# The last two output chunks of a hybrid attention layer as a pair in seven block products

## What is computed

```python
def hybrid_layer(x, cos, sin, w_in, ...):
    h = rmsnorm(x, g_norm)
    proj = jnp.einsum('bsd,de->bse', h, w_in)
    ...
    y_moba = rmsnorm(o_moba * jax.nn.silu(m_z), g_out_moba)
    ...
    y_nsa = rmsnorm(o_nsa * jax.nn.silu(n_z), g_out_nsa)
    y = jnp.concatenate([y_moba, y_nsa], axis=-1)
    return x + jnp.einsum('bse,ed->bsd', y, w_out)

def reference(x, ...):
    x = hybrid_layer(...)
    return rmsnorm(x, g_final)
```

## Time and profile before

| | before |
|---|---|
| median of 3 runs | 498.31 us |
| lowest, highest | 498.20, 498.56 us |
| the profiled execution | 498.54 us |
| its span | 496.7 us |
| matmuls and transposes in the program of TensorE | 1947 rows of its order |
| TensorE busy | 487.2 us (98%) |
| VectorE busy | 335.6 us (68%) |
| ScalarE busy | 250.5 us (50%) |
| GpSimd busy | 60.9 us (12%) |
| read from HBM | 93.93 MB |

### The profile page before, as it was taken

One profiled execution on the slowest core, in us unless ns is written; L12 is line 12 of the kernel. 1 busy time (PEld: TensorE's weight loads), 2 busy tenths in 40 slices (PEclk: granted clock), 3 DMA queues, 4 the chain that ended last, 5 costly groups with the idle time before them and its releaser, 6 DMA issues.

```text
span 496.7 us, 6459 instructions
## 1 busy us (share of the span) xinstructions
PE 487.2 (98%) x2512; PEld 405.4 (82%) x2512; DVE 335.6 (68%) x535; ACT 250.5 (50%) x358; POOL 60.9 (12%) x66
## 2 busy tenths in 40 slices
PE   8999999999999999999999999999999999999993
PEld 7888788787788888888888888888888888888882
DVE  5887544345879948766587878666888766765442
ACT  5884335353556535544544464665664544545421
POOL 2340101000102202000020200000323131022020
PEclk9999999999999999999999999999999999999998
DMA  8989788585353452443443734346257577367222
...
DMA packets 54543, 96.45 MB, mean 194 GB/s; under 512 B 4368, under 2 KB 13168, under 8 KB 54128
## 3 DMA queue, kind: packets, MB, share of 16 engines
...
HBM read 93.93 MB, written 2.10 MB: 193 GB/s over the span
## 4 chain that ended last, share of the span: by engine, by line
PE 95%; issue 2%; DMA 1%; DVE 0%; ACT 0%; ACTq 0%; POOLq 0%; POOL 0%; DVEq 0%
PE proj L647 26%; PE proj L649 25%; PE proj L648 25%; PE b_o L941 4%; PE b_t L628 2%; PE b_p L910 2%; PE b_s L810 2%; PE proj L680 2%; PE proj L686 1%; PE proj L691 1%; DMA xo<-in_x_dram 1%; PE b_s L649 1%; PE b_s L647 1%; PE b_s L648 1%; PE b_p L628 0%
## 5 line engine op out<-in xcount | busy, mean ns | idle before, releaser
L1341 DVE TENSOR_TENSOR w_lo<-w_raw,w_hi 128x2048 fp32r<-128x2048 f32 x68 | 157.5, 2319 | 87.6 <-ACT w_hi L1018 87.4
L647 PE MATMUL proj<-w_hi,xT_hi 128*128 128x512 f32 x484 | 191.0, 395 | 0.0
L649 PE MATMUL proj<-w_hi,xT_lo 128*128 128x512 f32 x484 | 188.8, 390 | 0.0
L648 PE MATMUL proj<-w_lo,xT_hi 128*128 128x512 f32 x484 | 188.6, 390 | 0.0
L1018 ACT ACTIVATE w_hi<-w_raw 128x2048 fp32r<-128x2048 f32 x68 | 129.7, 1911 | 34.9 <-PE proj L649 24.5
L647 PEld LDWEIGHTS proj<-w_hi,xT_hi 128*128 128x128 f32 x484 | 90.9, 188 | 20.1 <-issue 1.6
L649 PEld LDWEIGHTS proj<-w_hi,xT_lo 128*128 128x128 f32 x484 | 90.9, 188 | 19.4
L648 PEld LDWEIGHTS proj<-w_lo,xT_hi 128*128 128x128 f32 x484 | 91.0, 188 | 17.8
L1155 ACT ACTIVATE pT<-b_p 128x512 f32<-128x512 f32 (+2 forms) x24 | 11.7, 489 | 53.9 <-PE b_p L910 53.9
L595 POOL TENSOR_TENSOR rope_a<-rope_a,rope_b 128x512 f32<-128x512 f32 (+1 forms) x12 | 13.1, 1109 | 160.8 <-DVE rope_b L1428 160.8
L647 PE MATMUL proj<-w_hi,ymT_hi 128*128 128x512 f32 x80 | 31.2, 390 | 0.0
...
## 6 DMA issues: line engine op xcount, KB each, us to landing
...
```

Source lines behind the costliest of these rows:

```text
L647: nc.tensor.matmul(dst, a_hi, b_hi, start=first, stop=False, skip_group_check=goes_on)
L648: nc.tensor.matmul(dst, a_hi, b_lo, start=False, stop=False, skip_group_check=goes_on)
L649: return nc.tensor.matmul(dst, a_lo, b_hi, start=False, stop=last, skip_group_check=goes_on)
L1341: nc.vector.tensor_tensor(wl, w_raw[:, u % RAW], wh.bitcast(F32), ALU.subtract).then_inc(lo_ready, 1)
```

## The change

Output chunks 2 and 3 become the third pair. Their first units (2, 0) and (3, 0), 48 matmuls, are replaced by seven block products of 6 matmuls, with sums of y's blocks in the place of x's. For that, chunk 0's last unit moves ahead of both of chunk 1's; the blocks of the weights are loaded by SyncE, rounded by ScalarE and VectorE; y's sums are formed by VectorE in slot 60 (`y_sums`), rounded by ScalarE in slot 62 (`ys_round`) and their lo made by VectorE in slot 64 (`ys_residual`). The four copies of banks go to `rope_b` and `prob`, and VectorE adds them to the sum in memory (`mid_add`). `last_chunk` keeps the two units (3, 2) and (3, 3). Cut to its core:

```diff
-OUT_UNITS = [(0, 0), (0, 1), (1, 0), (1, 1), (0, 2), (1, 2), (0, 3), (1, 3)] + [(c, g) for c in (2, 3) for g in range(4)]
+OUT_UNITS = [(0, 0), (0, 1), (1, 0), (1, 1), (0, 2), (0, 3), (1, 2), (1, 3)]
+NSLOT = NPROJ + 16
+OUT_DONE = [65, 67, 71]
+PAIRS = [(11, 12), (13, 14), (NC + 2, NC + 3)]
+Z_PAIRS = 2
+FIRST_BLOCKS, T2_SLOT, EARLY, MIDDLE_BLOCKS, LATE_BLOCKS = [40, 48, 65], [41, 49, 66], [42, 50, 66], [42, 50, 67], [43, 51, 68]
+MIDDLE, LATE = [44, 52, 68], [45, 53, 69]
...
-    for c, g in OUT_UNITS:
+    for c, g in OUT_UNITS[:-1]:
         plain(NC + c, g)
+    a, b = PAIRS[2]
+    ring.append(("early", 2))
+    plain(NC + OUT_UNITS[-1][0], OUT_UNITS[-1][1])
+    ring.append(("middle", 2))
+    plain(a, 1)
+    ring.append(("late", 2))
+    for c, g in ((a, 2), (a, 3), (b, 1), (b, 2), (b, 3)):
+        plain(c, g)
...
+              66: 63, 67: 64, 68: 65, 69: 66, 70: 67, 71: 68, 72: 69}
...
+        ys = raw_e[:, :, :].rearrange("p m c -> p (m c)").rearrange("p (k t) -> p k t", k=UK)
+        ys_hi, ys_lo = xT_hi[:, NH:NH + UK, :], xT_lo[:, NH:NH + UK, :]
...
+                if u == 61:
+                    sp.wait_ge(blk_lo, 14)
+                    block(2, 0)
+                    block(2, 1)
+                if u == 63:
+                    block(2, 3)
+                if u == 65:
+                    sp.wait_ge(xs_lo_ok, 2)
+                    block(2, 2)
...
-                pe.wait_ge(xs_lo_ok, 1)
+                pe.wait_ge(xs_lo_ok, 1 if p < Z_PAIRS else 2)
...
-                bank_free(NC + 3)
                 for m in range(MT):
-                    for g in range(UPC):
+                    for u in (NU - 2, NU - 1):
...
+            def ys_round():
+                act.wait_ge(xs_ok, 2)
+                act.wait_ge(unit_used, used(UNIT_NO[NC - 1, 2]))
+                nc.scalar.activation(ys_hi, ys, ACT.Copy).then_inc(xs_hi_ok, 1)
...
+                if p == 2:
+                    act.wait_ge(y_done, 8)
+                    nc.scalar.activation(mid_copy(p, i), mid_bank(p, i)[:, :], ACT.Copy).then_inc(mid_out, 1)
+                    return
...
+                    if slot == MIDDLE[p]:
+                        if p == 2:
+                            block_hi(p, 4)
+                            block_hi(p, 5)
                         mid_out_(p, 2)
...
+            def mid_add(i):
+                m, c = ((0, 3), (1, 2), (0, 2), (1, 3))[i]
+                dve.wait_ge(mid_out, 4 * 2 + i + 1)
+                a = acc[:, m, c * CW:(c + 1) * CW]
+                nc.vector.tensor_tensor(a, mid_copy(2, i), a, ALU.add).then_inc(mid_added, 1)
+            def y_sums():
+                dve.wait_ge(ylo_done, 2)
...
+                step(nc.vector.tensor_tensor(ys, ymT_hi[:, 0:UK, :].bitcast(F32), ymT_lo[:, 0:UK, :].bitcast(F32), ALU.add), 5)
+                step(nc.vector.tensor_tensor(d, c, d, ALU.add), 6)
+                step(nc.vector.tensor_tensor(c, a, c, ALU.subtract), 7)
+                step(nc.vector.tensor_tensor(a, d, a, ALU.subtract), 8)
+                nc.vector.tensor_tensor(b, b, a, ALU.subtract).then_inc(xs_ok, 1)
...
+                if slot == LATE_BLOCKS[2]:
+                    block_lo(2, 4)
+                    block_lo(2, 5)
...
+                if slot == 60:
+                    y_sums()
+                if slot == MIDDLE_BLOCKS[2]:
+                    t4(2)
+                for i, at in enumerate((68, 68, 69, 70)):
+                    if slot == at:
+                        mid_add(i)
```

More of the change, by code:

```diff
@@ L78, in stream @@
     plain(first - 1, 3)
-    for p, (a, b, _) in enumerate(PAIRS):
+    for p, (a, b) in enumerate(PAIRS[:Z_PAIRS]):
         ring.append(("middle", p))
@@ L124, in rounded_at @@
         return slot + 2
-    return ROUNDED_AT.get(slot) if slot < 60 else slot - 2
-OUT_SLOT = OUT_DONE[:2] + [OUT_DONE[2] + 2]
+    return slot - 2 if 60 <= slot < 65 else ROUNDED_AT.get(slot)
+OUT_SLOT = OUT_DONE
 RAW, SPL = 3, 3
@@ L727, in seven @@
                 pe.wait_ge(blk_lo, 7 * p + n + 1)
-                xh, xl = [t[:, k0:k0 + 2, m * P:(m + 1) * P] for t in (xT_hi, xT_lo)] if of == "x" else                          [t[:, m, k0:k0 + 2, :] for t in (xs_hi, xs_lo)]
+                if of == "s" and p < Z_PAIRS:
+                    xh, xl = [t[:, m, k0:k0 + 2, :] for t in (xs_hi, xs_lo)]
+                else:
+                    pair = (ys_hi, ys_lo) if of == "s" else (xT_hi, xT_lo) if p < Z_PAIRS else (ymT_hi, ymT_lo)
+                    xh, xl = [t[:, k0:k0 + 2, m * P:(m + 1) * P] for t in pair]
                 wh, wl = block_split(p, n)
@@ L757, in last_chunk @@
             def last_chunk():
[L759 removed]
                 for m in range(MT):
[L761 removed]
+                    for u in (NU - 2, NU - 1):
                         if m == 0:
[L763 removed]
+                            pe.wait_ge(lo_ready, u - FIRST + 1)
                         for k in range(UK):
[L765 removed]
+                            last = three_products(*operands(u, m, k), False, u == NU - 1 and k == UK - 1, True)
                     last.then_inc(last_done, 1)
@@ L970, in _ @@
                 for p in range(len(PAIRS)):
-                    if slot == PAIRS[p][2] - 2:
+                    if slot == EARLY[p] and p < Z_PAIRS:
                         pair_early(p)
-                    if slot == PAIRS[p][2]:
+                    if slot == MIDDLE[p]:
                         pair_middle(p)
-                    if slot == PAIRS[p][2] + 1:
+                    if slot == LATE[p]:
                         pair_late(p)
@@ L978, in _ @@
                     unit(unit_at(slot))
+                if slot == EARLY[2]:
+                    pair_early(2)
                 if slot == 2:
@@ L1239, in _ @@
                     xs_round()
+                if slot == 62:
+                    ys_round()
                 for p in range(len(PAIRS)):
-                    s0 = PAIRS[p][2]
-                    if slot == s0 - 4:
+                    if slot == FIRST_BLOCKS[p]:
                         block_hi(p, 0)
                         block_hi(p, 1)
-                    if slot == s0 - 2 and p:
+                    if slot == MIDDLE_BLOCKS[p] and p:
                         block_hi(p, 2)
@@ L1290, in _ @@
                     prob_out(JOB_AT[slot - 2])
-                for p in range(len(PAIRS)):
-                    if slot == PAIRS[p][2] - 1:
-                        block_hi(p, 4)
-                        block_hi(p, 5)
+                if slot in LATE_BLOCKS[:Z_PAIRS]:
+                    for n in (4, 5):
+                        block_hi(LATE_BLOCKS.index(slot), n)
                 if slot % UPC == UPC - 1 and slot < NPROJ and ACT_READS[KINDS[slot // UPC]]:
@@ L1689, in _ @@
                     xs_residual()
+                if slot == 64:
+                    ys_residual()
                 for p in range(len(PAIRS)):
-                    s0 = PAIRS[p][2]
-                    if slot == s0 - 4:
+                    if slot == FIRST_BLOCKS[p]:
                         block_lo(p, 0)
@@ L1743, in _ @@
                     row_max(JOB_AT[slot])
-                for p in range(len(PAIRS)):
-                    if slot == PAIRS[p][2] - 1:
-                        block_lo(p, 4)
-                        block_lo(p, 5)
+                if slot in LATE_BLOCKS[:Z_PAIRS]:
+                    for n in (4, 5):
+                        block_lo(LATE_BLOCKS.index(slot), n)
                 if slot % UPC == UPC - 1 and slot < NPROJ and KINDS[slot // UPC] == "z":
```

71 lines of the change are left out of this document (39 added, 32 removed).

## The result

| | before | with the change |
|---|---|---|
| median | 498.33 us (4 executions) | 503.86 us (4 executions) |
| lowest, highest | 498.20, 498.56 us | 503.71, 503.88 us (the other three) |
| TensorE busy | 487.2 us | 487.8 us |
| VectorE busy | 335.6 us | 351.7 us |
| ScalarE busy | 250.5 us | 256.5 us |

The ratio is 1.0109, with a 95% interval of 1.0090 to 1.0129: 5.5 us slower, where 6.7 had been forecast (505.0, range 500 to 508).

The account below looks back on a forecast made before the run. TensorE, busy 98% of the span, was taken to bound the kernel; -1.36 us for six matmuls, five waits, restarts, 0.58 for GpSimd and 0.8 for y's sums made +6.7 us: 498.31 to 505.0 us, range 500 to 508.

Parts of the forecast that it names:

- first wait: Ahead of unit (0, 3), now a slot earlier: TensorE waits 1.13 us for the last part of y.
- y's sums: VectorE's slot 60: five sums, held up by GpSimd, make the last part of y 0.8 us late (0 to 1.35).
- second wait: Ahead of unit (1, 3): its hi stands behind ScalarE's squares of chunk 0, so TensorE waits 0.81 us.
- third wait: Ahead of unit (2, 1): its lo comes after TensorE wants it, a wait of 0.17 us.
- fourth wait: Ahead of P7: fifth block's lo and P6's copy come late, the largest wait, 3.15 us.
- fifth wait: Ahead of P4: the seventh block's lo ends after TensorE wants it, a wait of 0.91 us.
- restarts: TensorE after each of five waits: the second matmul starts later than usual, costing 0.11 us each.
- rival 3: TensorE's clock falls in the wait ahead of P7; slow matmuls cost 1.5 to 3 us more, 507.3; chance 0.13.
- the tail after the last matmul is the same work as before: After TensorE's last matmul: the remaining work is unchanged, so no time is added or taken away.
- the squares stand in front of the fifth block: ScalarE's program order: squares of chunk 1 run 454.53 to 456.08, ahead of the fifth block's rounding, ending 457.22.
- GpSimd's 0.58: Fifth block's lo on VectorE: GpSimd's second multiplication for chunk 1 keeps it waiting 0.58 us (0 to 0.58).
- What would show it: Signs in the trace: TensorE's busy time falls, five gaps appear, the first of y's sums takes 2.3 us.

Follow-up runs that it names:

- e9_as_is_again: The change unaltered, timed in more rounds beside the kernel with 16 added matmuls; 503.75 us, its profiled execution 503.89 us.
- e8_all: The change with y's second-half factor on ScalarE, both chunks' squares later, VectorE's block lo's and chunk 1's sums earlier; 496.60 us, 0.9966 of before.
- e6: On top of e2, the norm's factor on y's second half moved from VectorE's slot 61 to ScalarE's slot 62; 500.80 us.
- e2: The change with ScalarE's squares of chunk 1 moved behind the fifth and sixth block's roundings and P6's copy; 502.12 us.
- e7: On top of e2, ScalarE's squares of chunk 0 moved behind the hi of unit (1, 3); 500.16 us.
- e10_fill_again: The change with 16 matmuls that nobody reads in TensorE's wait ahead of P7, second timing; 502.81 us.
- e1_as_is: The change unaltered, for a second look at its trace; 504.55 us, its profiled execution 505.20 us.

## Why the prediction was right, and where it was not

The forecast of 505.0 against 503.86 comes from the right mechanism, but a part of the agreement is luck: terms that were too large stand against a fall of the clock that the sum did not have. Step by step, from the distances of starts in e9_as_is_again:

| term | forecast | measured |
|---|---|---|
| six matmuls less | -1.36 | -1.36 (e8_all: -1.5 of busy time) |
| first wait, ahead of (0, 3) | 1.13 | 1.27, with the sums' 0.24 in it |
| y's sums | 0.8 | 0.24, counted in the first wait |
| second wait, ahead of (1, 3) | 0.81 | 0.70 |
| third wait | 0.17 | 0 |
| fourth wait, ahead of P7, and GpSimd | 3.15 + 0.58 | 3.39 |
| fifth wait, ahead of P4 | 0.91 | 0 |
| restarts | 0.55 | 0.27 |
| slow matmuls behind the fourth wait | (rival 3) | 1.60 |
| after VectorE's last operation | 0 | -0.4 |
| sum | 6.7 | 5.5 |

The last matmul releases VectorE at 494.58 instead of 488.78, and the forecast had 495.5. The span grew by 5.4 only, because the tail got shorter: 502.1 - 494.58 = 7.5 against 496.7 - 488.78 = 7.9. VectorE's work in the tail takes 3.3 us in both. From its end to the end of the span, when the last rows are stored, it is 4.63 us in the trace before and 4.14 to 4.24 in nine traces of kernels with the change (all but e6's). So the step "the tail after the last matmul is the same work as before" holds for the engines and not for the time; why the end is shorter stays open.

- **The first, second and fourth waits** came where they were forecast. The first was 1.27 instead of 1.13 + 0.8, the second 0.70 instead of 0.81, and the fourth 3.39 instead of 3.15 and a part of 0.58. e2, e6 and e7 each moved what the step had named as the cause of one of them, and gained 1.7 (against 503.86), 1.3 and 2.0 us. e2 moved only ScalarE's two squares, so the step "the squares stand in front of the fifth block" is shown.
- **y's sums** were mis-sized, 0.8 instead of 0.24. The step that failed is "if each gets its turn between two sums, up to 0.2 + 0.2 + 0.7 more are lost", of which 0.55 was taken. The row that had made me fear it, 2.26 us for a small GpSimd operation beside a lo, is GpSimd waiting for VectorE: it ends at 377.05, just after VectorE's lo, which ends at 376.99. What did come is the first sum's 1.1, most of which VectorE's idle time took up. The Trainium skill (SBUF — State Buffer, "SBUF: two separate sides") says that whichever engine starts first holds the shared ports for its whole instruction; by that rule a small GpSimd operation costs VectorE at most its own length, and the trace agrees: VectorE's gaps are 0.03 us, and GpSimd's three operations are the ones that took longer, by 0.11 to 0.19 us.
- **GpSimd's 0.58** is there: the fifth block's lo took 1.87 instead of 1.22, 0.65 more. The 3.15 went by P6's copy at 458.75, and the lo was forecast at 458.47; with the 0.58 it would have ended at 459.05, which makes the fourth wait 3.45 and leaves 0.28 for the next. Measured were 3.39.
- **Rival 3 came true in both profiled executions**, and by the times in most of the others, where I had given it 0.13. The step that failed is "the wait is shorter than the idle time after which the clock fell here". The forecast wait with GpSimd's part in it (3.45) was itself above those 3.2 us, and one trace was no bound: the time from TensorE's last matmul to the fall at the end of the span differs from trace to trace. It is 3.4 us before, 2.4 in e9_as_is_again (last matmul 494.15, granted clock 1.00 up to 496.5 and 0.74 from 496.5 to 497.0), 4.3 in e10_fill_again and 5.0 in e1_as_is, and a wait of 3.39 lies among these. The cost, 1.60, is at the low end of my 1.5 to 3, and its net price is less: with slow matmuls TensorE comes to P4 when its lo is there, so there was no fifth wait (with the fill it was 0.23). That is a part of why e10 gained only 0.94.
- **Without the clock's fall** the change takes 502.8 to 503.1 us, some 2 us under the forecast. So about 1 us of the closeness of the point value is owed to the fall, which the sum did not have. Of the 2 us, 0.8 was asked for y's sums, 0.7 is the fifth wait (0.23 instead of 0.91) and 0.4 the tail; the third and fourth wait and the restarts gave less than forecast too, and the first wait 0.14 more.
- **What would show it**, as the prediction put it: the gaps ahead of (0, 3), (1, 3) and P7 and the 2.3 us of the first sum were seen (the first gap 1.4 us with its restart, not 2), the busy time of TensorE did not fall (the clock), and the gap ahead of P4 was seen only where the clock held.

Why the clock fell in some executions and not in others stays open, and so does what makes the start of some late; no run here varied either.
